# Split attention: near works of one pair of heads take turns with wide works of the next

## What is computed

```
A_PATTERNS = ((128, 1), (512, 4), (2048, 16))
def dilated_mixture(q, k, v):
    results = [dilated_band_attention(q, k, v, w, d) for (w, d) in A_PATTERNS]
    outs = jnp.stack([o for (o, _) in results], axis=0)
    lses = jnp.stack([l for (_, l) in results], axis=0)
    wts = jax.nn.softmax(lses, axis=0)
    return jnp.einsum('pbsh,pbshc->bshc', wts.astype(q.dtype), outs)
```

## Time and profile before

| what | value |
|---|---|
| median of three runs | 4514.96 us (4512.73 to 4517.98) |
| profiled execution, its own time | 4518.71 us |
| span of its trace | 4516.9 us |
| mean granted clock of TensorE | 0.934 |
| the stage in that trace | 311.4 us to 514.6 us |
| engines over the span | PE 88%, DVE 59%, ACT 38%, POOL 8% |

### The profile page before, as it was taken

How to read it: one execution, slowest core, us unless ns; L and a number is a source line. 1 busy time by engine, 2 the same in 40 slices (tenths; PEclk the granted TensorE clock), 3 DMA queues, 4 the chain that set the end, 5 groups by cost and what they waited for, 6 DMA issues and landing times. The chain is left out here.

```text
span 4516.9 us, 78685 instructions
## 1 busy us (share of the span) xinstructions
PE 3961.9 (88%) x32694; PEld 3251.6 (72%) x32694; DVE 2673.8 (59%) x4543; ACT 1710.3 (38%) x2993; POOL 353.9 (8%) x443
## 2 busy tenths in 40 slices
PE   6998788998897999799389899989999587999997
PEld 5887666877785667488377777878888466888886
DVE  3246648875674554798446113767888643655656
ACT  3037525773563442477437211223332112222222
POOL 0000101210000000121000000023333001000000
PEclk9999998998999999799789999978999798999998
DMA  3111339982000002899400211100000220111111
GB/s 104 42 57 41 110 149 352 396 328 92 13 2 1 1 25 88 334 396 396 155 21 2 84 56 62 30 9 3 3 4 4 100 112 28 47 47 56 38 47 42
DMA packets 162909, 437.72 MB, mean 97 GB/s; under 512 B 18964, under 2 KB 73116, under 8 KB 137980
## 3 DMA queue, kind: packets, MB, share of 16 engines
q1 hardware_dynamic: 153340, 399.13, 23.3%
q0 software_dynamic: 9216, 33.56, 2.9%
HBM read 379.07 MB, written 53.48 MB: 96 GB/s over the span
## 5 line engine op out<-in xcount | busy, mean ns | idle before, releaser
L562 PE MATMUL psum<-weight_parts,h_parts 128*128 128x512 f32 (+2 forms) x2880 | 598.7, 370 | 29.3 <-DVE h_parts L725 16.6
L562 PEld LDWEIGHTS psum<-weight_parts,h_parts 128*128 128x128 f32 x2880 | 506.6, 191 | 115.5 <-DVE weight_parts L710 13.2
L1810 DVE TENSOR_TENSOR weight_parts<-weights_raw,weight_parts 128x2048 fp32r<-128x2048 f32 x192 | 431.9, 2289 | 70.4 <-ACT weight_parts L1779 69.3
L1779 ACT ACTIVATE weight_parts<-weights_raw 128x2048 fp32r<-128x2048 f32 x192 | 360.3, 1919 | 95.2 <-DMA weights_raw<-in_moe_w_up 45.3
L1716 PE MATMUL psum<-weight_parts,picked_parts 128*128 128x512 f32 x1536 | 364.0, 397 | 9.4 <-DVE picked_parts L1797 9.4
L2194 PE MATMUL psum<-h_parts,up_parts 128*128 128x512 f32 x1536 | 354.1, 392 | 11.0 <-DVE up_parts L2269 11.0
L2210 PE MATMUL psum<-down_parts,hidden_parts 128*128 128x512 f32 x1536 | 352.7, 390 | 6.7 <-DVE down_parts L2274 6.7
L1716 PEld LDWEIGHTS psum<-weight_parts,picked_parts 128*128 128x128 f32 x1536 | 290.5, 191 | 73.1 <-DVE picked_parts L1797 12.6
L2194 PEld LDWEIGHTS psum<-h_parts,up_parts 128*128 128x128 f32 x1536 | 290.4, 189 | 72.4 <-DVE up_parts L2269 11.8
L710 DVE TENSOR_TENSOR weight_parts<-weights_raw,weight_parts 128x2048 fp32r<-128x2048 f32 (+2 forms) x48 | 100.7, 2098 | 406.3 <-ACT weight_parts L617 406.2
L2210 PEld LDWEIGHTS psum<-down_parts,hidden_parts 128*128 128x128 f32 x1536 | 289.5, 189 | 67.5 <-DVE down_parts L2274 7.1
(11 more groups left out here) (470 smaller groups left out, 7145.6 us busy)
## 6 DMA issues: line engine op xcount, KB each, us to landing
weights_raw<-in_moe_w_gate SPq DMA_DIRECT2D x64, 1024.0 KB, 13.5
weights_raw<-in_moe_w_up SPq DMA_DIRECT2D x64, 1024.0 KB, 14.0
weights_raw<-in_moe_w_down SPq DMA_DIRECT2D x64, 1024.0 KB, 13.0
w_ada<-in_w_ada SPq DMA_DIRECT2D x12, 2048.0 KB, 8.8
up_raw<-in_w_mlp_up SPq DMA_DIRECT2D x16, 1024.0 KB, 7.6
down_raw<-in_w_mlp_down SPq DMA_DIRECT2D x16, 1024.0 KB, 5.5
weights_raw<-in_even_w_in SPq DMA_DIRECT2D x10, 1024.0 KB, 5.1
weights_raw<-in_w_in SPq DMA_DIRECT2D x10, 1024.0 KB, 5.5
```

The source lines that it names most:

```text
L562: last = pe.matmul(ps[:, t, 0:width(n)], cols[:, i, KP * h + k, t * P:(t + 1) * P], part[:, n % 2, j, k, 0:width(n)], start=(h == 0 and m ...
L1779: act.activation(part[:, n % PART_SLOTS, 0], raw[:, n % RAW_SLOTS], ACT.Copy).then_inc(high, 1)
L1810: dve.tensor_tensor(part[:, n % PART_SLOTS, 1], raw[:, n % RAW_SLOTS], part[:, n % PART_SLOTS, 0].bitcast(F32), ALU.subtract).then_inc(low, 1)
```

## The change

The order of the works is new: four wide works of pair 0; then, for p = 1 to 5, the works of the pairs take turns, wide work j of pair p and then near work j of pair p - 1, for j = 0 to 3; at last the four near works of pair 5. So works 0 to 3 are wide, 4 to 43 alternate with the even ones wide, and 44 to 47 are near. The blocks of values come in the order in which the works first need them, in the same three slots. The statistics are moved once for each pair (16 DMAs, six times), and a near work of pair p waits for the moves of pairs 0 to p. The rest carries the new numbers through the semaphores.

```
--- before.py
+++ after.py
@@ -1018,33 +1019,46 @@
     st = c.at("softmax_stats", stats_kb + 1.5, [P, 4, 4, 2, 2])
     spare = lambda k: ag[:, k, A_WIDTH:D]
     near_out, near_part, wide_part = [[spare(k), spare(k + 1)] for k in (0, 2, 4)]
+    own = lambda a, i: a[part(i) % 2]
     wide_out = lambda p: vz[:, :, p * P:(p + 1) * P]
     half = [slice(0, 64), slice(64, 128)]
-    WIDE = 4 * PAIRS
-    N = 2 * WIDE
-    near = lambda i: i >= WIDE
-    pair = lambda i: (i % WIDE) // 4
-    tiles = lambda i: (2 * (i % 4), 2 * (i % 4) + 1)
+    works = [(0, 0, j) for j in range(4)]
+    for p in range(1, PAIRS):
+        works += [w for j in range(4) for w in ((0, p, j), (1, p - 1, j))]
+    works += [(1, PAIRS - 1, j) for j in range(4)]
+    N = len(works)
+    number = {w: i for i, w in enumerate(works)}
+    near = lambda i: works[i][0] == 1
+    pair = lambda i: works[i][1]
+    part = lambda i: works[i][2]
+    tiles = lambda i: (2 * part(i), 2 * part(i) + 1)
+    nears = [i for i in range(N) if near(i)]
     first_key = lambda t: min(max(P * t - 64, 0), S - 256)
     kind_of = lambda t: 0 if t == 0 else 2 if t == TILES - 1 else 1
 
     ring = []
     for i in range(N):
-        ring += ([("out", i - 2)] if i - 2 >= WIDE else []) + [(i, 0), (i, 1)]
+        ring += ([("out", i - 2)] if i >= 2 and near(i - 2) else []) + [(i, 0), (i, 1)]
     ring += [("out", N - 2), ("out", N - 1)]
     place = {entry: g for g, entry in enumerate(ring)}
     owner = lambda e: "out" if e[0] == "out" else "act" if e[1] == 0 or near(e[0]) else "dve"
     taken = [sum(1 for e in ring[:g + 1] if owner(e) == owner(entry)) for g, entry in enumerate(ring)]
-    by_act = lambda i: 2 * (i + 1) - min(i + 1, WIDE)
-    by_dve = lambda i: min(i + 1, WIDE)
-    outs = lambda i: max(0, i - WIDE)
-
-    slot_of = lambda i: pair(i) if not near(i) else PAIRS + (i - WIDE) // 2
-    last_use = lambda n: 4 * n + 4 if n < PAIRS else WIDE + 2 * (n - PAIRS) + 2
-    loads_of = lambda n: 2 if n < PAIRS else 8
+    by_dve = lambda i: sum(1 for v in range(i + 1) if not near(v))
+    by_act = lambda i: 2 * (i + 1) - by_dve(i)
+    outs = lambda i: sum(1 for v in nears if v < i)
+    two_before = lambda i: sorted(v for v in nears if v < i)[-2] if outs(i) >= 2 else None
+
+    blocks = []
+    for i in range(N):
+        b = (1, pair(i), part(i) // 2) if near(i) else (0, pair(i), 0)
+        if b not in blocks:
+            blocks.append(b)
+    slot_of = lambda i: blocks.index((1, pair(i), part(i) // 2) if near(i) else (0, pair(i), 0))
+    last_use = lambda n: max(i for i in range(N) if slot_of(i) == n) + 1
+    loads_of = lambda n: 2 if blocks[n][0] == 0 else 8
     landed = lambda n: 16 * sum(loads_of(k) for k in range(n % SLOTS, n + 1, SLOTS))
     rows = dram["h_scratch"]
-    stats_at = lambda i: wide_st[:, i % 4, :, pair(i)]
+    stats_at = lambda i: wide_st[:, part(i), :, pair(i)]
 
     with stage(nc, "scores_ready", "scores_taken", "probs_ready", "ring_turned", "act_turned", "dve_turned", "weighted",
                "out_copied", "out_taken", "out_written", "bias_loaded", "values_loaded_0", "values_loaded_1",
@@ -1060,12 +1074,13 @@
                 if n >= SLOTS:
                     sp.wait_ge(weighted, last_use(n - SLOTS))
                 to, sem = v_b[:, n % SLOTS], values_loaded[n % SLOTS]
-                if n < PAIRS:
+                kind, p, q = blocks[n]
+                if kind == 0:
                     for h in (0, 1):
-                        source = rows[512 * h:512 * h + 512, n * P:(n + 1) * P].rearrange("(j r) d -> j r d", r=4)
+                        source = rows[512 * h:512 * h + 512, p * P:(p + 1) * P].rearrange("(j r) d -> j r d", r=4)
                         sp.dma_start(to.rearrange("p (r h) d -> p r h d", h=2)[:, :, h], source).then_inc(sem, 16)
                     return
-                p, t0 = (n - PAIRS) // 2, 4 * ((n - PAIRS) % 2)
+                t0 = 4 * q
                 for t in range(t0, t0 + 4):
                     keys = rows[first_key(t):first_key(t) + 256, p * P:(p + 1) * P]
                     for r in (0, 1):
@@ -1073,7 +1088,7 @@
                                      keys.rearrange("(m c r) d -> r m c d", c=2, r=2)[r]).then_inc(sem, 16)
 
             def move_stats(p0, p1):
-                sp.wait_ge(probs_ready, 16 * p1)
+                sp.wait_ge(probs_ready, 4 * number[0, p1 - 1, 3] + 4)
                 for r in range(4):
                     for b in range(4):
                         sp.dma_start(near_st[r:P:4, b:TILES:4, p0:p1].rearrange("i h p a k -> i h (p a k)"),
@@ -1081,15 +1096,12 @@
                           .then_inc(stats_moved, 16)
 
             sp.dma_start(bias[:], dram["const_even_bias"]).then_inc(bias_loaded, 16)
-            for n in range(PAIRS):
+            for n in range(SLOTS):
                 load_values(n)
-            for n in range(PAIRS, PAIRS + 2):
-                load_values(n)
-            move_stats(0, PAIRS - 1)
-            load_values(PAIRS + 2)
-            move_stats(PAIRS - 1, PAIRS)
-            for n in range(PAIRS + 3, 3 * PAIRS):
-                load_values(n)
+            for p in range(PAIRS):
+                move_stats(p, p + 1)
+                for n in range(SLOTS + 3 * p, min(SLOTS + 3 * p + 3, len(blocks))):
+                    load_values(n)
             sp.wait_ge(bias_loaded, 16)
 
         @block.tensor
@@ -1109,7 +1121,7 @@
                                                  qkT[half[a], x, p, t * P:(t + 1) * P], keys[:, :, m0:m0 + 64],
                                                  start=(m == 0), stop=(m == 2))
                             else:
-                                r = i % 4
+                                r = part(i)
                                 last = pe.matmul(out, qkT[half[a], x, p, 512 * u + r:512 * u + 512:4], keys[:, r],
                                                  start=(m == 0), stop=(m == 2))
                 last.then_inc(scores_ready, 1)
@@ -1139,7 +1151,7 @@
                     pe.wait_ge(out_copied, i)
                 for u in (0, 1):
                     for ch in (0, 1):
-                        v = v_b[:, n % SLOTS, (4 * (i % 2) + 2 * u if near(i) else 2 * (i % 4)) + ch]
+                        v = v_b[:, n % SLOTS, (4 * (part(i) % 2) + 2 * u if near(i) else 2 * part(i)) + ch]
                         for a in (0, 1):
                             last = pe.matmul(ps[half[a], 7, u * P:(u + 1) * P], v[:, half[a]], pt_b[:, u, a, ch],
                                              start=(ch == 0), stop=(ch == 1))
@@ -1149,7 +1161,7 @@
                 pe.wait_ge(out_copied, i + 1)
                 bank = slot_free(place["out", i])
                 for u, t in enumerate(tiles(i)):
-                    pe.transpose(bank[:, u * P:(u + 1) * P], near_out[i % 2][:, u * P:(u + 1) * P], c.ident[:])
+                    pe.transpose(bank[:, u * P:(u + 1) * P], own(near_out, i)[:, u * P:(u + 1) * P], c.ident[:])
                     last = pe.transpose(bank[:, (2 + u) * P:(3 + u) * P], wide_out(pair(i))[:, t], c.ident[:])
                 last.then_inc(turned, 1)
 
@@ -1159,7 +1171,7 @@
                     scores(i + 1)
                 if i >= 1:
                     weigh(i - 1)
-                if i - 2 >= WIDE:
+                if i >= 2 and near(i - 2):
                     turn_out(i - 2)
                 turn(i)
             turn_out(N - 2)
@@ -1188,11 +1200,11 @@
             def out_cols(i):
                 act.wait_ge(weighted, i + 1)
                 if near(i):
-                    if i - 2 >= WIDE:
-                        act.wait_ge(turned, place["out", i - 2] + 1)
-                    act.activation(near_out[i % 2], ps[:, 7, 0:256], ACT.Copy).then_inc(out_copied, 1)
+                    if two_before(i) is not None:
+                        act.wait_ge(turned, place["out", two_before(i)] + 1)
+                    act.activation(own(near_out, i), ps[:, 7, 0:256], ACT.Copy).then_inc(out_copied, 1)
                 else:
-                    to = wide_out(pair(i)).rearrange("p t (i r) -> p t i r", r=4)[:, :, :, i % 4]
+                    to = wide_out(pair(i)).rearrange("p t (i r) -> p t i r", r=4)[:, :, :, part(i)]
                     act.activation(to, ps[:, 7, 0:256].rearrange("p (t i) -> p t i", t=TILES), ACT.Copy)\
                        .then_inc(out_copied, 1)
 
@@ -1222,7 +1234,7 @@
                     dve.wait_ge(bias_loaded, 16)
                 ts = tiles(i)
                 if near(i):
-                    dve.wait_ge(stats_moved, 16 * (16 if pair(i) < PAIRS - 1 else 32))
+                    dve.wait_ge(stats_moved, 16 * 16 * (pair(i) + 1))
                     step(dve.tensor_copy(s_b[:, i % 2, :, :, 0], near_st[:, ts[0]:ts[0] + 2, pair(i), :, 0]))
                 for u, t in enumerate(ts):
                     for a in (0, 1):
@@ -1262,18 +1274,18 @@
                     dve.wait_ge(out_written, outs(i) - 1)
                 bank = ps[:, 4 + g % 3, :]
```

(16 more changed lines are left out.)

50 lines of the change are left out of this document (24 added, 26 removed).

## The result

The changed kernel takes 4615.42 us (median of 4 runs, 4605.36 to 4626.3) against 4516.47 us for the kernel before on the same chip: ratio 1.022, 95% interval 1.0193 to 1.0248. It is slower, by 87 to 112 us. The forecast was 4610 us.

What follows compares the result with a forecast made beforehand. It took PE as the wide half's limit and DVE as the near half's. First wait's end 340.6, four rounds of 48.1 and the tail gave stage end 610.1, 95.5 us later: 4515 + 95 = 4610 us, range 4590 to 4630.

Steps and rivals of the forecast that it cites:

- The stall behind SP's wait: On SP after weigh(b + 6): loads and move hold the statistics back 19.1 us, a stall of 16.6 us.
- The first wait and the last: DVE's waits in lowest(5) and lowest(44): 7.2 and about 21 us, ending at 340.6 and 585.5 us.
- The refill and the rounds: From a wait's end to the end of weigh(b + 14): 29.05 us; a round of eight works takes 48.1 us.
- The order gives nothing: In the alternating works: a wide and a near step together take 7.7 us, against 7.66 us before.
- The sum: The stage ends at 610.1 us against 514.6 us before, 95.5 us later, giving 4610 us.
- A: Rival on SP: moves are in time, only lowest(5) waits; 4507 us, or 4495 us with pairs at 7.1; chance 0.04.
- B: Rival on SP: issues at half of 0.65 us, each of five waits 8 us shorter; 4570 us; chance 0.05.
- C: Rival on SP: each DMA waits for the one before, a move takes 28.8 us; 4713 us; chance 0.01.
- D: Rival after each wait: a slower refill, 3 us more in each of six; 4628 us; chance 0.06.
- The clock's price: On PE after a wait: weigh, turn and near scores at half clock take 5.04 us, costing 2.0 us a round.

Runs made afterwards that it cites:

- one_move: The changed kernel with only pair 0's statistics moved and used by all near works (other pairs' results wrong): stage 203.2 us, time 4521.0 us, ratio 1.0009.
- one_move_copies: one_move with ACT's copies put ahead of the second half of the next work's exponentials: stage 189.0 us, time 4506.0 us, ratio 0.9978.
- first: The changed kernel with SP issuing each move of statistics ahead of the loads that wait for weigh: stage 233.7 us, time 4554.6 us, ratio 1.0075.
- turns: The changed kernel with each move made two DMAs through DRAM and put ahead of the loads: stage 199.2 us, time 4518.3 us, ratio 0.9993.
- early: The kernel before, its order of works kept, with statistics moved pair by pair after each pair's last wide work: stage 191.6 us, time 4510.4 us, ratio 0.9981.
- early_copies: early with ACT's copies put ahead of the second half of the next work's exponentials: stage 191.1 us, time 4503.8 us, ratio 0.9965.

## Why the prediction was right, by its steps

- *The stall behind SP's wait.* Right, in place, number and size. Forecast: 19.1 us from the end of weigh(b + 6) to the end of the wait, DVE idle 16.6. Measured: 18.1 from the first issue (19.05 forecast), DVE idle 15.5 to 16.2. The near block was issued in 5.14 us where I took 6.08 from the first of two such rows; the other has 5.06. That is the 1 us. Why the first took longer is not shown.
- *The first wait and the last.* They end at 340.41 (340.6 forecast) and at 584.02 (585.5 forecast). DVE is idle for 9.03 and 23.50 us where I said 7.2 and about 21. The first counts from the end of DVE's last copy at 331.38, and I had counted from the 333.4 of the earlier trace rows. Only the ends of the waits enter the sum.
- *The refill and the rounds.* 29.05 us forecast; measured 418.25 - 388.17 = 30.1. The refill came out as forecast, but for 1 us: weigh of the work that waited starts 397.93 - 388.17 = 9.8 us after the wait, 8.8 forecast, because the transposes of `turn_out(11)` come between, at half clock, which the one wait of before did not have in its way. The pairs took 7.77 for 7.7. A round is right to 0.1 us since the two errors, 1 us each, cancel; that is luck.
- *The order gives nothing.* Right, shown by one_move, and its reason, ACT's copies behind the next exponentials, by one_move_copies.
- *The sum.* The stage's end was forecast 95.5 us later; the stage became 94.3 us longer. The median rose by 99 us; the other 5 us or so lie outside the stage, which the forecast did not touch.
- *Rivals.* A needed a wait-free SP; first and turns show that it takes another list, and even then the time is that of before. B (issues at half the price) and C (DMAs one after another) fall with the 10.4 to 11.2 us for 16 DMAs in every move. The section of the Trainium skill that C cites ("DMA: Bandwidth & Descriptors", Anatomy of one DMA) gives its 2 us for DMAs issued by GpSimd; those of SP here land after 1.8 us. D, a slower refill, was 1 us a round and was met by the shorter stall.
- *The clock's price.* Too small. From 391.83 to 397.93 PE takes 6.10 us for what takes 2.5 + 1.0 us at full clock, so a refill loses 2.6 us and not the 2.0 of the rows, since `turn_out` is in it too. The Trainium skill, "TensorE: Matmul & The Clock Gate", Terms, gave an estimate of 2.3 us for a refill of 4.5 us; for these 6.10 us the same rule gives an estimate of about 3 us, and the trace agrees with it to half a microsecond.

What stays open: why the granted clock of the later, unchanged part differs from kernel to kernel (0.98 to 1.00 before, 0.93 to 0.96 after).

## What to carry to other kernels

When a list of DMAs mixes loads that wait for a buffer with transfers that are ready, put the ready ones first: all that stands behind a wait on that queue is late, and here a copy of 16 KB stopped PE, ACT and DVE for 16 us at a time. Price a group of small DMAs by their issue time (here 0.65 us each) and not by bytes; two DMAs through DRAM beat sixteen direct ones. Before works of two kinds are interleaved to even out the engines, write down for one step which instruction of each engine the next engine waits for: here the loads of a pair of steps were more even than in either half (PE 7.1, ACT 6.2, DVE 5.9 us), and the gain was hidden behind the order of two instructions on ACT.

## What the runs showed that I had not expected

A transfer to DRAM and back in pieces of 16 bytes, with SP waiting in between, took 6.25 us against 11.7 for the sixteen direct DMAs. And the 96 small DMAs of early and early_copies left no mark on the loads beside them: the near blocks of early were issued in 5.11 us each, as in the kernel after.
